# Even layer: another product order, the index products in a second line of side work, and one run of 16 attention units

## The reference, cut to what matters

```
aq, ak, av, bq, bk, bv, iq, ik, iw = _split_cols(h @ w_in, EVEN_SIZES)
aq, ak = rms_norm per head;  bq, bk = rms_norm per head
ya = diff attention: softmax(aq0 ak0) - lam * softmax(aq1 ak1), times av      # 4 heads, causal
ya = rms_norm(ya, subln_a) * (1 - lam_init)
score = sum over 8 heads of relu(iq . ik / 8) * iw, causal                    # the index products
sel = top_k(score, 64)
yb = attention of bq with bk, bv over the selected keys only                  # 8 heads
return concatenate([ya, yb])                                                   # then times w_out
```

## Time and profile before

| | |
|---|---|
| median of 3 runs | 1421.41 us (1421.3 to 1422.6) |
| the profiled execution's own time | 1419.48 us |
| its span | 1417.8 us |
| PE busy | 1169.2 us (82%), 7659 matmuls |
| weight loads | 857.0 us (60%) |
| DVE busy | 631.1 us (45%), 1281 instructions |
| ACT busy | 483.1 us (34%) |
| mean granted TensorE clock | 0.894 |
| chain that ended last | PE 53%, DMA 22%, DVE 16%, ACT 5% |

### The profile page before, as it was taken

One profiled execution on the slowest core, in us unless ns is written; L12 is line 12 of the kernel. 1 busy time (PEld: TensorE's weight loads), 2 busy tenths in 40 slices (PEclk: granted clock), 3 DMA queues, 4 the chain that ended last, 5 costly groups with the idle time before them and its releaser, 6 DMA issues.

```text
span 1417.8 us, 19477 instructions
## 1 busy us (share of the span) xinstructions
PE 1169.2 (82%) x7659; PEld 857.0 (60%) x7659; DVE 631.1 (45%) x1281; ACT 483.1 (34%) x783; POOL 7.6 (1%) x54
## 2 busy tenths in 40 slices
PE   7889878667576675766997788999999998999998
PEld 6665665234232341323774448899997646999986
DVE  5745552001001010003844576765545676775543
ACT  5544511000000000003623245554434456565441
POOL 1000000000000000000000000000000000000000
PEclk9997879889887898878997569999999989999999
DMA  8635459999999999999465332856455680855420
GB/s 304 239 122 189 182 220 411 428 431 430 429 429 429 430 429 431 428 420 386 151 224 191 119 120 88 270 178 239 178 208 179 234 300 2 282 181 188 183 90 30
DMA packets 121775, 368.65 MB, mean 260 GB/s; under 512 B 9890, under 2 KB 56141, under 8 KB 110926
## 3 DMA queue, kind: packets, MB, share of 16 engines
q1 hardware_dynamic: 120604, 367.26, 67.5%
q10 hardware_dynamic: 1074, 0.08, 0.1%
HBM read 366.28 MB, written 1.05 MB: 259 GB/s over the span
## 4 chain that ended last, share of the span: by engine, by line
PE 53%; DMA 22%; DVE 16%; ACT 5%; issue 3%; SPq 1%; DVEq 0%; ACTq 0%
PE ps L1925 51%; DMA more<-in_w_up_dram 8%; DMA more<-in_w_down_dram 6%; DMA more<-in_w_gate_dram 6%; DVE ring_r L33 3%; PE ps L1929 3%; DVE st L33 3%; DVE R_c L33 2%; DVE X_c L33 1%; DVE R_c_r L33 1%; DMA ring<-in_ada_w_dram 1%; DVE sc L33 1%; DVE R_a L33 1%; SPq L688 1%; DVE x L33 1%
## 5 line engine op out<-in xcount | busy, mean ns | idle before, releaser
L1925 PE MATMUL ps<-ring,xg 128*32 128x512 f32 x640 | 139.7, 734 | 126.3 <-DMA more<-in_w_gate_dram 78.5
L1925 PE MATMUL ps<-hT_r,ring_r 128*128 128x256 f32 x800 | 224.6, 281 | 0.0
L1925 PEld LDWEIGHTS ps<-ring,xg 128*32 128x32 f32 x640 | 36.8, 132 | 222.1 <-issue 222.1
L1925 PE MATMUL ps<-R_c_r,W_c_r 128*128 128x256 f32 (+1 forms) x624 | 154.5, 284 | 0.0
L33 DVE TENSOR_TENSOR ring_r<-ring,W_c_r 128x1024 fp32r<-128x1024 f32 x94 | 115.2, 1225 | 86.9 <-ACT W_c_r L33 82.4
L1925 PEld LDWEIGHTS ps<-hT_r,ring_r 128*128 128x128 f32 x800 | 152.4, 191 | 0.0
L1925 PE MATMUL ps<-R_c_r,X_c_r 128*128 128x256 f32 (+1 forms) x624 | 151.0, 283 | 0.6 <-DVE R_c_r L33 0.4
L33 DVE TENSOR_TENSOR ring_r<-ring,X_c_r 128x1024 fp32r<-128x1024 f32 x88 | 107.8, 1225 | 86.8 <-ACT X_c_r L33 83.5
L1925 PE MATMUL ps<-more,xg 128*32 128x512 f32 x384 | 134.2, 721 | 0.0
L33 ACT ACTIVATE W_c_r<-ring 128x1024 fp32r<-128x1024 f32 x94 | 99.6, 1060 | 75.9 <-PE ps L1925 70.4
L33 DVE TENSOR_TENSOR x<-x,ps 128x512 f32<-128x512 f32 x36 | 24.8, 688 | 218.4 <-PE ps L1925 218.1
(11 more groups left out here) (293 smaller groups left out, 1916.7 us busy)
## 6 DMA issues: line engine op xcount, KB each, us to landing
ring<-in_ada_w_dram SPq DMA_DIRECT2D x24, 2048.0 KB, 8.4
ring<-in_w_gate_dram SPq DMA_DIRECT2D x20, 2048.0 KB, 16.6
ring<-in_w_up_dram SPq DMA_DIRECT2D x20, 2048.0 KB, 18.6
ring<-in_w_down_dram SPq DMA_DIRECT2D x20, 2048.0 KB, 17.6
more<-in_w_gate_dram SPq DMA_DIRECT2D x12, 2048.0 KB, 26.5
more<-in_w_up_dram SPq DMA_DIRECT2D x12, 2048.0 KB, 27.5
more<-in_w_down_dram SPq DMA_DIRECT2D x12, 2048.0 KB, 26.5
ring<-in_ffn_gate_dram SPq DMA_DIRECT2D x22, 1024.0 KB, 5.5
```

The costliest lines, as they stand in the source:

```text
L1925: return pe.matmul(out, lhsT, rhs, start=start, stop=stop, skip_group_check=True)
```

## The change

The plan's order becomes kvi, tli, bq, ak, aq, av. The index products get a list of side work of their own (`idx`), of which each call and each unit does one step beside the two steps of `side`; it is filled when the side work of tli is done. They use banks 6 and 7 and two relu buffers (in `hn` and in the part of `kvi` that has been turned). The turns of bq and iq use both banks too. The two attention runs become one of 16 units, with `until` at units 8 and 12. The close of the layer's first modulation product keeps its place in front of tli, and tli is now the second product: the close is at call 4. POOL only has the two masks left.

```diff
 class Feed:
@@
         self.side.go(2)
+        self.idx.go(1)
         self.fed.append(i)
@@ def make_plan
-    k = p.load("w", "ak")
+    k = p.load("w", "kvi")
     for q in range(3):
         p.feed(k, q)
     p.ada(("n", 0, 0))
     p.feed(k, 3)
-    for name in ("aq", "av", "kvi"):
-        p.product(name, 4)
     p.close(("f", len(p.chunks)))
     p.product("tli", 2)
     p.ada(("f", len(p.chunks)))
     p.product("bq", 4)
     p.close(("f", len(p.chunks) - 1))
-    p.units(2, 8, (0, 2, 4, 6))
-    p.units(3, 8, (0, 2, 4, 6), 2, 1)
+    for name in ("ak", "aq", "av"):
+        p.product(name, 4)
+    p.units(2, 16, (0, 2, 4, 6, 8, 10, 12, 14), 10, 1)
@@
-        sco, wrk, rel = R1c[:, 6144:6400], R1c[:, 6400:6656], R1c[:, 6656:7168]
+        sco, wrk = hn[:, 0, 512:768], hn[:, 0, 768:1024]
+        rel = [two(hn[:, 1, 512:1024], 2), kvi[:, :, 128:384]]
@@ attend, in all engines
                 side.go(beside)
-                if n == 3 and u == 4:
-                    side.until(ev, "sel1")
+                idx.go(1)
+                if n == 2 and u in (8, 12):
+                    idx.until(ev, f"sel{u // 4 - 2}")
@@ scalar, indexer
-                    act.wait_ge(s_ix, 8 * a + 2 * hp + 2)
-                    if a or hp:
-                        act.wait_ge(s_iw, 4 * a + hp)
-                    S(act_op, rel[:, 0:2 * w], ps[7][:, 0:2 * w], ACT.Relu, up=s_rl)
+                    n = 4 * a + hp
+                    act.wait_ge(s_ix, 2 * n + 2)
+                    if n >= 2:
+                        act.wait_ge(s_iw, n - 1)
+                    for i in range(2):
+                        S(act_op, rel[n % 2][:, i, 0:w], ps[6 + i][:, 0:w], ACT.Relu, up=s_rl if i else None)
@@ tensor
+            def indexer(a):
+                for hp in range(4):
+                    take(6, 7)
+                    pe.wait_ge(s_hv, 8)
+                    for i in range(2):
+                        mm(ps[6 + i][:, 0:w], iqT[...], ikT[...], True, True).then_inc(s_ix, 1)
+                    free[6] = free[7] = C.next(s_rl)
+                    yield
+                yield from steps(5)
+                ev.add(f"sel{a}")
+            def work_tli():
+                yield
+                pe.wait_ge(s_ev, 12)
+                headturn(kvi[:, :, 128:512], 3, [6, 7])
+                yield
+                pe.wait_ge(s_ik, 1)
+                headturn(tli[:, :, 56:184], 1, [6])
+                headturn(ikd, 1, [7])
+                yield
+                idx.add(indexer(0))
+                idx.add(indexer(1))
             def work_bq():
                 pe.wait_ge(s_kd, 2)
                 headturn(kd, 1, [7])
                 yield from steps(4)
-                pe.wait_ge(s_hd, 7)
-                headturn(bq, 4, [7])
-                ev.add("bT")
-                yield
-                yield from indexer(0)
-                yield from indexer(1)
+                pe.wait_ge(s_hd, 5)
+                headturn(bq, 4, [6, 7])
+                yield
+            def work_ak():
+                yield from steps(4)
+                pe.wait_ge(s_hd, 6)
+                headturn(ak, 4, [6, 7])
+                yield
+            def work_aq():
+                yield from steps(5)
                 pe.wait_ge(s_hd, 7)
+                headturn(aq, 4, [6, 7])
@@
             feed.drain()
-            side.until(ev, "qk")
-            attend(2, 2, {0: [(s_hv, 8), (s_ev, 16), (s_lam, 1)]})
-            side.add(steps(5))
-            side.until(ev, "sel0", "bT")
-            attend(3, 2, {0: [(s_hv, 15), (s_ev, 18)]})
             side.end()
+            attend(2, 2, {0: [(s_hv, 15), (s_lam, 1)], 2: [(s_ev, 22)]})
```

More of the change, by code:

```diff
@@ L78, with __init__ @@
 class Feed:
-    def __init__(self, begin, side, use=None, lag=2):
+    def __init__(self, begin, side, use=None, lag=2, idx=None):
         self.begin, self.side, self.use, self.lag, self.fed, self.then = begin, side, use, lag, [], {}
+        self.idx = idx or Side()
         self.begun = set()
@@ L207, in make_plan @@
                 p.experts.append(p.load("moe", name, g, q))
-    k = p.load("w", "ak")
-    p.first["ak"] = len(p.chunks)
+    k = p.load("w", "kvi")
+    p.first["kvi"] = len(p.chunks)
     for q in range(3):
@@ L773, in gpsimd @@
             G(pool.memset, at, 0.0, up=s_slopes)
-            ev = set()
-            def then_av():
-                ev.add("qk")
-                yield
-            def indexer(a):
+            for a in range(2):
                 w = 128 * (a + 1)
-                yield from steps(4)
                 pool.wait_ge(s_iw, 4 * a + 4)
@@ L1073, in scalar @@
                     overflow()
-            feed = Feed(lambda i: begin(i, XFc), side, lag=5)
+            feed = Feed(lambda i: begin(i, XFc), side, lag=5, idx=idx)
             for q in range(2):
[L1077 to L1089, removed]
+                feed.ahead(first["kvi"] + q)
             def indexer(a):
@@ L1309, in headturn, with attend @@
                         V(ts, o, p, gain, scale, ALU.mult, ALU.mult, up=s_hv)
-            def attend(n, beside, chunks=(), XF=None):
+            def attend(n, beside, chunks=(), XF=None, work={}):
                 at_n = attns[n]
@@ L1319, in scores @@
                 def scores(u):
+                    if u in work:
+                        side.add(work[u]())
                     side.go(beside)
-                    if n == 3 and u == 4:
-                        side.until(ev, "sel1")
+                    idx.go(1)
+                    if n == 2 and u in (8, 12):
+                        idx.until(ev, f"sel{u // 4 - 2}")
                     ada(("u", n, u))
@@ L1787, in vector @@
                 feed(i)
-            feed.product(first["aq"], 4, ends(work_aq()))
-            feed.product(first["av"], 4, ends(work_av()))
-            feed.product(first["kvi"], 4, ends(work_kvi()))
             feed.product(first["tli"], 2, ends(work_tli()))
             feed.product(first["bq"], 4, ends(work_bq()))
+            feed.product(first["ak"], 4, ends(work_ak()))
+            feed.product(first["aq"], 4, ends(work_aq()))
+            feed.product(first["av"], 4, lambda: None)
             feed.drain()
-            side.until(ev, "qk")
-            attend(2, 2)
+            side.end()
             def work_sub():
@@ L1803, in work_sub @@
                     yield
-            side.add(work_sub())
-            side.until(ev, "sel0", "bT")
-            attend(3, 2, [first["wo", 1], first["wo", 1] + 1], XFc)
+            attend(2, 2, [first["wo", 1], first["wo", 1] + 1], XFc, {12: work_sub})
             side.end()
@@ L2551, in tensor, with work_aq @@
+            def work_aq():
+                yield from steps(5)
+                pe.wait_ge(s_hd, 7)
+                headturn(aq, 4, [6, 7])
+            feed = Feed(begin, side, use, lag=5, idx=idx)
             for q in range(4):
-                how[first["ak"] + q] = ([0, 1], 512, q, q == 3, hH, hL_at, XFc, 20)
-            feed.then[first["ak"] + 3] = ends(work_ak())
-            for i in range(first["ak"], first["ak"] + 4):
-                if i == first["ak"] + 2:
+                how[first["kvi"] + q] = ([0, 1], 512, q, q == 3, hH, hL_at, XFc, 20)
@@ L2556, in tensor @@
+            feed.then[first["kvi"] + 3] = ends(steps(3))
+            for i in range(first["kvi"], first["kvi"] + 4):
+                if i == first["kvi"] + 2:
                     modulated(0, lambda: ada(("n", 0, 0)))
                 feed(i)
-            product(feed, "aq", [2, 3], hH, hL_at, XFc, ends(work_aq()))
-            product(feed, "av", [4, 5], hH, hL_at, XFc, ends(work_av()))
-            product(feed, "kvi", [0, 1], hH, hL_at, XFc, ends(steps(3)))
             product(feed, "tli", [2, 3], hH, hL_at, XFc, ends(work_tli()), n=256)
```

153 lines of the change are left out of this document (44 added, 109 removed).

## The result

The changed kernel takes 1426.8 us (median of 6 runs, 1426.0 to 1430.1) against 1421.4 for the kernel before (6 runs): ratio 1.0042, 95% interval 1.0029 to 1.0054, so it is slower by some 5 us. On another chip it was 1424.7 (10 runs) against 1420.5: 1.0024 (1.0007 to 1.0041). The forecast was 1420.7, no change that could be told. 1426.8 lies inside the range given, at the upper end of the forecast's own 1414 to 1427, but the kernel is slower by more than the runs scatter.

What follows compares the result with a forecast made beforehand. PE was taken to bound the products, and no single engine the attention (round trips PE, ACT, DVE). Products +43.4 and attention -44.1 gave -0.7 on 1419.48 us, as a median 1420.7; range 1407 to 1433.

Steps and rivals of the forecast that it cites:

- What bounds the stages, and the attention: Products bound by PE, attention by round trips of PE, ACT, DVE; attention 65.4 us instead of 109.5, -44.1.
- Rivals 2 and 3: Attention: without a gap at full clock, -10, 1411 us, chance 0.16; or staying at half clock, +10, 1431, chance 0.17.
- The close in front of the first product: Start of products: the close in call 4 waits for ACT's copy of acc; first product +11.8 us, sum +11.0.
- The waits: Products: PE waits where a turn and an index step or norm stand too close, and in the drain; 27.4 us.
- Call 12: Products, tli's turn: waits for ak's late load, conversions and DVE's copies before the index step; 6.9 us.
- Call 15: Products, index step right behind kd's turn: waits for DVE's late copy of bkT; 4.0 us.
- Call 17: Products, bq's turn two chunks after bq's last: norm takes 15.1 us, 12 covered; wait 3.2 us.
- Call 21: Products, ak's turn: 12.2 us, 5.6 covered, wait 6.6; then 3.2 us for its copies before the index step.
- Rival 1: Products: waits 17 us instead of 27.4, with two restarts fewer; -13, 1407.5 us, chance 0.16.
- PE's added work: Products: turns of kd and bq and eight index steps now done there; +6.0 us (5 to 11).
- The restarts of the clock: Products: four pauses over 2.51 us each cost 1.6 us at half clock; +6.4 us (3.2 to 9.6).
- Rival 4: Products never back at full clock between pauses of calls 12 to 21 and the drain; +15, 1436 us, chance 0.07.

Runs made afterwards that it cites:

- e6_after: The kernel after, unchanged, on another chip and with a second profiled execution: 1424.7 us, ratio 1.0024 to the kernel before.
- e12_warm3: The kernel after with PE's waits at the first close and in calls 12, 15, 17, 21 filled with small unread products: 1416.7 us, ratio 0.9966.
- e5_before: The kernel before, unchanged, second profiled execution: products 78.8 us instead of 80.3; medians of before 1421.4 to 1422.0 and 1420.5 us.
- e4_idx_rest: The kernel after with one resting step in the index line between its third and fourth steps, on PE, ACT and DVE: 1422.2 us, ratio 1.0008.

## Why the prediction was wrong, point by point

- *What bounds the stages, and the attention*: right. -44.1 forecast, -44.6 measured, each of its four parts within 2.1 us. That the total, 65.4 against 65.3, is closer than its parts is luck: units 0 to 7 came out 2.0 shorter and units 8 to 15 1.4 longer. Rivals 2 and 3 did not come: the clock was 0.84 over the whole window and 0.87 in units 0 to 7, in between the two.
- *The close in front of the first product*: right in the wait, +11.8 forecast and +11.6 measured for the start of the first product. PE stood 11.69 us, and the close began 11.65 us behind DVE's first feature instruction, where the prediction's 679.1 is 11.5 behind it.
- *The waits*: right, each of them. Call 12: 6.9 forecast, 6.5 measured, with ak's late load in it. Call 15: 4.0 and 4.16. Call 17: 3.2 and 3.22. Call 21: 6.6 and 6.83, then 3.2 and 2.56. Sum 27.4 and 26.5; the 27.4 held aq's turn (1.1 us, PE's work, which the products of before have too), so for the waits alone it is 26.3 against 26.5. Rival 1 is out.
- *PE's added work*: 6.0 forecast; 7.8 is left of the 49.0 us when the other terms are taken off. The eight index steps took 5.8 us of it (4.5 forecast), part of them and of the turns at half clock.
- *The restarts of the clock*: this is the step that failed. I took one pause of before, 4.6 us until full clock and 1.6 us lost, and multiplied it by four, less 0.8 at the first product and less before's own. That makes +4.0 us at half clock (6.4 - 1.6 - 0.8). Measured: 12.7 and 11.6 against 3.9 and 3.3, +8.3 to +8.8. In the first profile 3.0 us were lost behind call 12, 2.5 behind call 15, 1.5 behind call 17 and 2.6 behind call 21, where 1.6 each was taken, and 2.7 at the first product. From the end of the last wait to the first product at full clock PE worked 7.0 us behind call 12 (716.30 to 723.33), 6.0 behind call 15, 4.1 behind call 17 and 6.4 behind call 21. So 4.6 was a fair value for a lone wait (calls 15 and 17), and the larger error was to count calls 12 and 21 as one pause each: a second wait (1.79, 2.56) stands inside, so that PE was at half clock from 713.4 to 723.3 and from 766.6 to 777.5. The first product, which I had let off with 0.8 less, was at half clock for 13 matmuls until 690.4, 9.6 us behind the start of the close (6.0 in e6_after). The miss of this term, 4.3 to 4.8 us, is nearly the miss of the stage (5.1 in the first pair of profiles). e12_warm3 confirms the cause: with PE kept at work in the same waits the kernel takes 1416.7.
- Rival 4 put the clock's extra cost at +15 and gave it 0.07. The truth lies between it and the forecast: the clock came back behind every pause, but behind two waits in a row later than in the one row that I had. The Trainium skill (TensorE: Matmul & The Clock Gate, "HAM oscillation — how this bites in real kernels") describes groups that each start slow behind a wait; the trace agrees for the waits of 3.2 us and more, and the clock fell behind 2.51 us in before too, but not behind 1.59 (e5_before).
- *The function table*: 1.28 us, and the exponential starts 0.01 us behind it (801.59, 802.88). The Trainium skill (ScalarE: Activation LUTs, "What ACT_TABLE_LOAD costs") gives 2.66 us for a switch; the added part does not show here behind the load.
- *Outside the stage*: nothing was forecast. In profiled executions the odd layer takes 2.8 us more and a later stretch of it 1.5 in some. How much of this is in the medians is open: the profiled executions of before lie 1.9 to 4.6 us under the medians of their runs, those of after 1.1 to 3.3 above, so the stretch may be slow in other executions of before as well. The stage alone is +3.9 between the means of the profiles, the medians are +5.4 and +4.3, so most of the loss is the stage's.

## What to carry to other kernels

A pause of PE can be priced twice: the wait, and the work behind it at half clock until the clock is back (behind 2.51 us in before and behind every wait of 3.2 us and more in the products here; waits of 1.4 and 1.59 us in before cost nothing more). A second short wait before that time can prolong it: counted from the start of the turn, PE was back at full clock after 10 to 11 us in calls 12 and 21 of after (6.3 at the least, in call 12 of e4_idx_rest), and after 3.9 to 6.0 behind the lone waits of calls 15, 17 and, in e4_idx_rest, 21. When a wait is moved by a call, follow the engine that ends it: here ACT's chain of features and then DVE's backlog of conversions decided, and of the calls tried for the close, 4, 6 and 8, only the last held no wait. In work that goes PE, DVE, PE, leave a chunk of other work between the turn and the step that reuses its bank; one `yield` in each engine's program was worth 2.5 to 4.6 us, and putting the turns of bq and ak a call later some 10 more (by subtraction: 1417.1 to 1402.4 for both; no run has the turns alone).

## What I had not expected of the hardware

Products that nobody reads made the kernel 8 to 11 us faster (e12_warm3), by holding PE's granted clock at 0.97 instead of 0.79 in a stage that is limited by PE in between its waits. And the same 160 PE instructions took 29.35 or 32.15 us according to whether the clock held behind a wait of 1.47 us or fell behind one of 1.99, the same in all three profiles of before and in both of after. Nearer to the change the profiles of one kernel do differ: at the first product the clock was back 3.9 or 5.7 us behind its start in before.
